# Newton's steps on VectorE for the inverse roots of a kernel's norms, and the last tile's squares summed on TensorE

## The chip, the cores and the metric

One core of a Trainium2 chip runs the whole kernel in one launch. The metric is device time in microseconds (us), the median over several executions. The core's engines are TensorE (PE in the profile; PEld is its weight load), VectorE (DVE), ScalarE (ACT), GpSimd (POOL) and SyncE (SP, which here only starts transfers). Each runs its instructions in order, and they wait for one another through semaphores.

## The reference

Two transformer blocks stand one behind the other, on 512 tokens of width 1024, all in fp32. The first has a chunked attention beside a short convolution, a mixture of 32 experts (two per token), and a gated projection of a side input. The second puts 16 meta tokens in front (528 tokens), and has a pooling mixer, a feed-forward layer, keys and values, a sliding-window attention and another feed-forward layer. What the change touches is the norm, which stands before and behind nearly each of these parts:

```python
def rms_norm(x, g):
    xf = x.astype(jnp.float32)
    y = xf * lax.rsqrt(jnp.mean(xf * xf, axis=-1, keepdims=True) + EPS)
    return (y * g.astype(jnp.float32)).astype(x.dtype)
```

For every token the squares of 1024 numbers are averaged, and the token is multiplied by the inverse root of that mean. The kernel does the matmuls of the large weights in three parts each (high and low halves of weights and data).

## The kernel before

**Layout.** Activations lie transposed: 8 tiles of 128 features, each with the tokens as columns (`hT`, `yT`: 128 x 8 x 528). Tokens are worked on in two halves, r = 0 and 1, of 272 and 256 columns (of 256 and 256 behind the meta tokens' last use). Weights stream through `raw` (SyncE's transfers), are cast to `whi` by ScalarE (L1675) and split to `wlo` by VectorE (L971); `tile` (L377) makes three matmuls for each piece (L388).

**A norm over features.** The features of a token are spread over partitions and tiles, so a norm (name `nm`, half `r`) takes a chain over all four engines:

1. ScalarE squares tile k as it comes (`square`, L1917), the first tile into the accumulator `zacc`, the others into one of three buffers `zsq`.
2. GpSimd adds each buffer to `zacc` (`accumulate`, L2199; L2204); for the second half of the pooling output VectorE does it (L1381).
3. TensorE sums `zacc` over partitions: for each 128 tokens one matmul against a column of ones (`columns`, L690, L697). The trace shows it as two instructions per column. The first half has three columns where the meta tokens are in it, else two.
4. VectorE makes the mean (L1395). ScalarE takes the square root (`root_act`, L355). VectorE takes the reciprocal (L345) and corrects it by one of Newton's steps, four small instructions (L347 to L353; `root`, L342). All of these work on 128 x 2 to 128 x 5 numbers.
5. VectorE writes the roots on a diagonal (L1401, L1402), TensorE spreads them over all partitions (`spread`, L700; L707 for the 16 meta tokens, L709 for the rest), ScalarE copies them to `rb` (L1972).
6. VectorE scales `yT` by `rb` (L1420), GpSimd (r = 0, L2262) or VectorE (r = 1, L1425) adds it to `hT`, ScalarE and VectorE make the high and low halves of the next matmul's input (L1964, L1430).

The fourteen norms of this kind are, by name, `mp0` (pooling output), `fp0` (before the first feed-forward), `fo0` (its output), `kv` (before the keys), `mp1` (attention output), `fp1` and `fo1`, with two halves each. Beside them there are the first norm of the input, by token, with four roots (`x`, L990), the router's (`n2`), the gate's (`ple`, its spread is L653) and the one before the pooling (`pre0`, whose roots scale a matrix, L1336, that TensorE uses at L683). That makes 21 roots. The attention's head norms take a square root of their own on ScalarE (L1714), which stays.

**Order.** Each engine's program is written out by hand. The main stream is the tiles of matmuls; the norms' steps are generators in a list (`Side`) that are advanced once per piece of a tile, so that a few matmuls stand between a column sum and its spread. Since each engine is in order, a step that waits stops all that stands behind it. On ScalarE, each change between a square root, an exponential, a sigmoid and Silu (L1990) puts a table load in front of the instruction.

Of the kernel before, what the change touches and what calls it, by code (L numbers as in the profile page):

```python
# [140 lines left out]
def _program(nc, ctx, T, out, marks):  # L141
# [119 lines left out]
    zsq = [pl(f"zsq{i}", [128, 272]) for i in range(3)]  # L261
    tmp = [pl(f"ztmp{i}", [128, 272]) for i in range(3)]
# [79 lines left out]
    def root(e, w, y, xm, u, name, *event):  # L342

        w.wait_ge(*at("sqrt", *event))
        e.reciprocal(y, y).then_inc(*hit(name))  # L345
        w.wait_ge(*last(name))
        e.tensor_tensor(u, y, y, ALU.mult).then_inc(*hit(name))  # L347
        w.wait_ge(*last(name))
        e.tensor_tensor(u, u, xm, ALU.mult).then_inc(*hit(name))
        w.wait_ge(*last(name))  # L350
        e.tensor_scalar(u, u, -0.5, 1.5, ALU.mult, ALU.add).then_inc(*hit(name))
        w.wait_ge(*last(name))
        e.tensor_tensor(y, y, u, ALU.mult).then_inc(*hit(name, ("root", *event)))  # L353

    def root_act(e, w, y, xm, *event):  # L355
        w.wait_ge(*at("mean", *event))
        e.activation(y, xm, ACT.Sqrt).then_inc(*hit("act_root", ("sqrt", *event)))
# [3 lines left out]
    def tensor(e):  # L361
# [328 lines left out]
        def columns(nm, r):  # L690

            c0 = RNG[nm][r][0]
            b = take(("col", nm, r), SIDE)
            w.wait_ge(*at("acc", nm, r, 7))
            for x, c in CH[r].items():
                if c >= c0:
                    p = e.matmul(b[:, x:x + 1], zacc[:, c:c + 128], ones[:, 0:1], start=True, stop=True)  # L697
            p.then_inc(*hit("pe_norm", ("col", nm, r)))
# [263 lines left out]
    def vector(e):  # L962
# [399 lines left out]
        def dve_pool():  # L1362
# [16 lines left out]
            accumulate("mp0", 1, 7)  # L1379
# [283 lines left out]
    def scalar(e):  # L1663
        w, side = per_engine(e)
        fed, nsq = [0], [0]
        sq_user = {}
# [17 lines left out]
        def act_load():  # L1684
# [4 lines left out]
            for i in range(4):  # L1689
                w.wait_ge(*at("x", i))  # L1690
                e.activation(xr[:, i, :], xt[:, i, :], ACT.Square, accum_out=xs[:, 1, i:i + 1]).then_inc(
                    *hit("act_sq", ("x sq", i)))
                root_act(e, w, xs[:, 0, i:i + 1], xs[:, 1, i:i + 1], "x", i)
# [120 lines left out]
        def act_route():  # L1814
# [8 lines left out]
            root_act(e, w, ns[:, 3, 0:4], ns[:, 2, 0:4], "n2")  # L1823
# [47 lines left out]
        def act_ple():  # L1871
# [18 lines left out]
            for m in range(8):  # L1890
                tile(J["pg"], m)
                if m == 0:
                    root_act(e, w, rcol[:, 0, 1:5], rcol[:, 1, 1:5], "ple")
                    w.wait_ge(*at("prb"))
                    e.copy(rb[:, MT:L], bk("prb")).then_inc(*hit("act_out", ("free", "prb"), ("ple rb",)))
# [9 lines left out]
            root_act(e, w, rcol[:, 0, 0:5], rcol[:, 1, 0:5], "pre0")  # L1905
# [11 lines left out]
        def square(nm, r, k, src, acc, sq):  # L1917

            c0, c1 = RNG[nm][r]
            if k == 0:  # L1920
                e.activation(acc[:, c0:c1], src[:, k, c0:c1], ACT.Square).then_inc(*hit("act_sq", ("acc", nm, r, 0)))
                return
# [27 lines left out]
        def act_post(nm, r, nev, g, off):  # L1950
# [3 lines left out]
            n0, n1 = cols(nm, r)  # L1954
            root_act(e, w, rcol[:, 0, n0:n1], rcol[:, 1, n0:n1], nm, r)
# [18 lines left out]
        def act_rooted(nm, r, wait):  # L1974
            for _ in range(wait):
                yield
            n0, n1 = cols(nm, r)
            root_act(e, w, rcol[:, 0, n0:n1], rcol[:, 1, n0:n1], nm, r)
            yield
            yield  # L1980
            rb_copy(nm, r)
# [214 lines left out]
    def gpsimd(e):  # L2196
# [56 lines left out]
        def pool_post(nm, r, nev):  # L2253
# [4 lines left out]
            for s in range(11):  # L2258
# [5 lines left out]
                if nev and 3 <= s < 10:  # L2264
                    accumulate(nev, r, s - 2, zacc, zsq)
                yield

        def pool_ffn(l, after):
# [7 lines left out]
            for r in range(2):  # L2276
                for m in range(8):
                    tile(J["fd", l, 1, r], m)
                    if m:
                        accumulate(f"fo{l}", r, m, zacc, zsq)  # L2280
# [66 lines left out]
        for k in range(1, 8):  # L2347
# [9 lines left out]
        for r in range(2):  # L2357
            for m in range(8):
                tile(J["wo2b", r], m)
                if m:  # L2360
# [190 lines left out]
```

## Time and profile before

| | |
|---|---|
| Time, median of 3 runs | 2228.89 us (2228.74 to 2229.91) |
| The profiled execution's own time | 2229.37 us |
| Its span, first to last instruction | 2227.6 us |
| Mean granted TensorE clock | 0.931 of full speed |
| TensorE busy | 1905.9 us, 86% of the span |
| VectorE busy | 849.0 us, 38% |
| ScalarE busy | 654.2 us, 29% |
| GpSimd busy | 240.2 us, 11% |

The profile is one execution. A share of busy time is an average over stages: from about 500 to 1000 us the experts' weights are transferred at some 400 GB/s and TensorE waits for them; in the rest it is TensorE's matmuls, stopped at times by a norm. In a list of waits the numbers are the total, how often, and the longest. In a timeline a row gives start and duration in us, engine, line, operation, output<-input, and in brackets how long the engine had been idle before it and what ended that.

### The profile page before, as it was taken

Reading aid. Unit: us, or ns where it says so; the run is one execution under the profiler, and the core shown is the slowest. Engines: PE = TensorE matmul, PEld = TensorE weight load, DVE = VectorE, ACT = ScalarE, POOL = GpSimd, SP = SyncE. Lnnn points to the kernel's source line nnn. Section 1 sums busy time; section 2 is a strip of 40 time slices with the busy share of each in tenths; the row PEclk is TensorE's granted clock in tenths of the full one; section 3 lists DMA queues with packets and bytes.
Section 4 is the critical chain, followed back from the end, with each engine's and each line's share of the span. In section 5 each row is a group of like instructions: output and inputs, shape, how many; then the busy total and the mean of one; then the engine's idle time right before and its main releaser. Section 6 shows DMA issues by size and latency. Waiting matters only on the chain.

```text
span 2227.6 us, 30483 instructions
## 1 busy us (share of the span) xinstructions
PE 1905.9 (86%) x13042; PEld 1563.1 (70%) x13042; DVE 849.0 (38%) x1433; ACT 654.2 (29%) x1195; POOL 240.2 (11%) x235
## 2 busy tenths in 40 slices
PE   6977999959877788767859999998978869999997
PEld 4754888635434334335759999997956759999997
DVE  4644325330000000006583332346655473432455
ACT  5333323301000000014453222234445543222233
POOL 0022000000000000002240000004212240000013
PEclk9998999969999989997979999998999979999998
DMA  6211342649999999984112332233311212232342
GB/s 217 85 48 48 97 170 85 272 145 401 398 395 394 394 405 407 402 335 147 57 38 67 93 98 85 91 97 120 111 39 57 68 56 81 93 104 84 95 141 87
DMA packets 64428, 368.09 MB, mean 165 GB/s; under 512 B 7665, under 2 KB 10353, under 8 KB 52001
## 3 DMA queue, kind: packets, MB, share of 16 engines
q1 hardware_dynamic: 52672, 335.57, 41.4%
q0 software_dynamic: 6032, 21.32, 2.9%
q10 hardware_dynamic: 5584, 9.21, 1.1%
q8 instruction: 105, 1.72, 0.3%
q14 instruction: 35, 0.28, 0.0%
HBM read 349.55 MB, written 16.52 MB: 164 GB/s over the span
## 4 chain that ended last, share of the span: by engine, by line
PE 62%; DMA 19%; DVE 10%; ACT 5%; POOL 2%; issue 2%; SPq 0%; POOLq 0%; ACTq 0%; DVEq 0%
PE bank L388 49%; DMA e<-in_we 17%; PE bank L563 3%; PE bank L581 2%; POOL zacc L2204 1%; ACT SS L2098 1%; PE bank L434 1%; DVE scr L1135 1%; DMA yg<-y_scratch,dst 1%; PE bank L709 1%; DVE SS L1563 1%; DVE sm L1570 1%; DVE ztmp L1420 1%; PE bank L774 1%; PE bank L816 1%
## 5 line engine op out<-in xcount | busy, mean ns | idle before, releaser
L388 PE MATMUL bank<-nhi,whi 128*128 128x256 f32 (+2 forms) x1568 | 457.4, 292 | 14.4 <-DVE nlo L1430 6.6
L388 PE MATMUL bank<-nlo,whi 128*128 128x256 f32 (+2 forms) x1568 | 452.0, 288 | 0.0
L388 PE MATMUL bank<-nhi,wlo 128*128 128x256 f32 (+2 forms) x1568 | 451.9, 288 | 0.0
L971 DVE TENSOR_TENSOR wlo<-raw,whi 128x1024 fp32r<-128x1024 f32 x243 | 304.3, 1259 | 143.8 <-ACT whi L1675 140.0
L388 PEld LDWEIGHTS bank<-nhi,whi 128*128 128x128 f32 x1568 | 303.3, 193 | 19.9 <-DVE yT L1615 7.0
L388 PEld LDWEIGHTS bank<-nlo,whi 128*128 128x128 f32 x1568 | 302.9, 193 | 0.9
L388 PEld LDWEIGHTS bank<-nhi,wlo 128*128 128x128 f32 x1568 | 302.1, 193 | 1.5
L1675 ACT CAST whi<-raw 128x1024 fp32r<-128x1024 f32 x243 | 252.9, 1042 | 143.0 <-PE bank L388 118.5
L563 PE MATMUL bank<-e,xT 128*64 128x256 f32 x2048 | 245.1, 394 | 48.0 <-DMA e<-in_we 38.3
L563 PEld LDWEIGHTS bank<-e,xT 128*64 128x64 f32 x2048 | 151.9, 142 | 146.9 <-DMA e<-in_we 53.9
L388 PE MATMUL bank<-ghi,whi 128*128 128x256 f32 (+1 forms) x704 | 202.5, 288 | 0.0
L388 PE MATMUL bank<-ghi,wlo 128*128 128x256 f32 (+1 forms) x704 | 200.9, 285 | 0.0
L388 PE MATMUL bank<-glo,whi 128*128 128x256 f32 (+1 forms) x704 | 200.7, 285 | 0.0
L1266 DVE TENSOR_TENSOR hb<-hb,bank 128x256 f32<-128x256 f32 x32 | 13.5, 421 | 465.2 <-PE bank L563 465.2
L581 PE MATMUL bank<-e,h 128*64 128x512 f32 x512 | 136.3, 682 | 50.0 <-DMA e<-in_we 49.4
L2204 POOL TENSOR_TENSOR zacc<-zacc,zsq 128x256 f32<-128x256 f32 (+1 forms) x91 | 90.3, 993 | 818.1 <-ACT zsq L1929 816.9
L388 PEld LDWEIGHTS bank<-ghi,whi 128*128 128x128 f32 x704 | 135.6, 193 | 0.0
L388 PEld LDWEIGHTS bank<-glo,whi 128*128 128x128 f32 x704 | 135.4, 192 | 0.0
L388 PEld LDWEIGHTS bank<-ghi,wlo 128*128 128x128 f32 x704 | 135.1, 192 | 0.0
L581 PEld LDWEIGHTS bank<-e,h 128*64 128x64 f32 x512 | 39.4, 154 | 131.1 <-issue 69.0
L388 PE MATMUL bank<-xhi,whi 128*128 128x512 f32 x288 | 122.2, 424 | 3.2 <-DVE wlo L971 3.2
L388 PE MATMUL bank<-xhi,wlo 128*128 128x512 f32 x288 | 114.4, 397 | 0.0
(305 smaller groups left out, 2530.7 us busy)
## 6 DMA issues: line engine op xcount, KB each, us to landing
e<-in_we SPq DMA_DIRECT2D x96, 2048.0 KB, 46.4
raw<-in_w_down SPq DMA_DIRECT2D x64, 512.0 KB, 3.6
raw<-in_w_gate SPq DMA_DIRECT2D x44, 512.0 KB, 3.5
raw<-in_w_up SPq DMA_DIRECT2D x44, 512.0 KB, 3.5
y_scratch<-ys ACTq DMA_DIRECT2D x64, 128.0 KB, 8.4
raw<-in_w_q SPq DMA_DIRECT2D x12, 512.0 KB, 4.0
B<-in_rel POOLq DMA_DIRECT2D x8, 512.0 KB, 4.4
raw<-in_w_gc SPq DMA_DIRECT2D x8, 512.0 KB, 4.1
```

The source lines that it names most:

```text
L388: i = e.matmul(o, a, x[:, k0 + k, c0:c1], start=(k == 0 and n == 0), stop=(k == j.K - 1 and n == 2))
L434: p = e.matmul(bs[i][:, 0:256], x[:, k, t], a, start=(k == 0 and n == 0), stop=(k == 7 and n == 2))
L563: p = e.matmul(b[64 * hf:64 * hf + 64, 0:256], xT[n % 2][:, k, :], W[:, k, 256 * hf:256 * hf + 256], start=(k == 0), stop=(k == 7))
L581: p = e.matmul(b[64 * nh:64 * nh + 64, :], h2[n % 2][:, 2 * (kc % 2) + kc // 2, :], W[:, kc, 512 * nh:512 * nh + 512], start=(kc == 0), st ...
L709: p = e.matmul(b[:, o + (i - m0) * 128:o + (i - m0 + 1) * 128], ones, dg[:, i - 1, :], start=True, stop=True)
L774: p = e.matmul(b[:, 0:128], x[:, k, c:c + 128], a, start=(k == 0 and n == 0), stop=(k == 7 and n == 2))
L816: p = e.matmul(bb[par][:, x * 256 + c0:(x + 1) * 256], qT[64 * par:64 * par + 64, h // 2, t * 128:(t + 1) * 128], kT[64 * par:64 * par + 6 ...
L971: e.tensor_tensor(wlo[u % NSP][:], raw[u % NRAW][:], whi[u % NSP][:].bitcast(F32), ALU.subtract).then_inc(*hit("dve_low", ("lo", u)))
L1135: op(*a, **kw).then_inc(*hit("dve_route", *ev))
L1420: e.scalar_tensor_tensor(x[:, 0:c1 - c0], yT[:, s, c0:c1], v1(name, 8 * l + s), rb[:, c0:c1], ALU.mult, ALU.mult).then_inc(*hit("dve_post" ...
L1675: e.copy(whi[u % NSP][:], raw[u % NRAW][:]).then_inc(*hit("act_high", ("hi", u)))
L2204: e.tensor_tensor(a, a, sq[marks.noted("sq", nm, r, k)][:, 0:c1 - c0], ALU.add).then_inc(*hit("pool_acc", ("acc", nm, r, k)))
```

## The change

Two things. The square root on ScalarE and the reciprocal go; `root` now starts from an integer estimate of the inverse root (the bits of the mean, halved and taken from a constant) and makes three of Newton's steps, of three instructions each, all on VectorE, at all 21 roots. And in the fourteen norms over features, ScalarE writes the squares of the eighth tile to one of two new buffers `zlast`, nobody adds them to `zacc`, and TensorE takes them in with a second matmul per column. `pre0`, which has its own accumulator, keeps its additions.

```diff
+    zlast = [pl(f"zlast{i}", [128, 272]) for i in range(2)]
...
     def root(e, w, y, xm, u, name, *event):
-        w.wait_ge(*at("sqrt", *event))
-        e.reciprocal(y, y).then_inc(*hit(name))
-        w.wait_ge(*last(name))
-        e.tensor_tensor(u, y, y, ALU.mult).then_inc(*hit(name))
-        w.wait_ge(*last(name))
-        e.tensor_tensor(u, u, xm, ALU.mult).then_inc(*hit(name))
-        w.wait_ge(*last(name))
-        e.tensor_scalar(u, u, -0.5, 1.5, ALU.mult, ALU.add).then_inc(*hit(name))
-        w.wait_ge(*last(name))
-        e.tensor_tensor(y, y, u, ALU.mult).then_inc(*hit(name, ("root", *event)))
-
-    def root_act(e, w, y, xm, *event):
         w.wait_ge(*at("mean", *event))
-        e.activation(y, xm, ACT.Sqrt).then_inc(*hit("act_root", ("sqrt", *event)))
+        e.tensor_scalar(y.bitcast(I32), xm.bitcast(I32), -0.5, 1597463007.0, ALU.mult, ALU.add).then_inc(*hit(name))
+        for n in range(3):
+            w.wait_ge(*last(name))
+            e.tensor_tensor(u, y, y, ALU.mult).then_inc(*hit(name))
+            w.wait_ge(*last(name))
+            e.scalar_tensor_tensor(u, u, -0.5, xm, ALU.mult, ALU.mult).then_inc(*hit(name))
+            w.wait_ge(*last(name))
+            e.scalar_tensor_tensor(y, u, 1.5, y, ALU.add, ALU.mult).then_inc(
+                *hit(name, *([("root", *event)] if n == 2 else [])))
...
         def columns(nm, r):
             c0 = RNG[nm][r][0]
             b = take(("col", nm, r), SIDE)
-            w.wait_ge(*at("acc", nm, r, 7))
+            w.wait_ge(*at("acc", nm, r, 6))
+            w.wait_ge(*at("sq", nm, r, 7))
+            sq = zlast[marks.noted("last", nm, r)]
             for x, c in CH[r].items():
                 if c >= c0:
-                    p = e.matmul(b[:, x:x + 1], zacc[:, c:c + 128], ones[:, 0:1], start=True, stop=True)
+                    e.matmul(b[:, x:x + 1], zacc[:, c:c + 128], ones[:, 0:1], start=True, stop=False)
+                    p = e.matmul(b[:, x:x + 1], sq[:, c - c0:c - c0 + 128], ones[:, 0:1], start=False, stop=True)
...
         def square(nm, r, k, src, acc, sq):
+            if k == 7 and nm != "pre0":
+                i = len(lasts) % 2
+                if len(lasts) >= 2:
+                    w.wait_ge(*at("col", *lasts[-2]))
+                lasts.append((nm, r))
+                marks.note(i, "last", nm, r)
+                e.activation(zlast[i][:, 0:c1 - c0], src[:, k, c0:c1], ACT.Square).then_inc(
+                    *hit("act_sq", ("sq", nm, r, k)))
+                return
...
-            root_act(e, w, rcol[:, 0, n0:n1], rcol[:, 1, n0:n1], nm, r)
...
-                if nev and 3 <= s < 10:
+                if nev and 3 <= s < 9:
                     accumulate(nev, r, s - 2, zacc, zsq)
...
-                    if m:
+                    if 1 <= m < 7:
                         accumulate(f"fo{l}", r, m, zacc, zsq)
```

`root_act` goes at all its six call sites. The additions of tile 7 go in the same way at the other three places (VectorE's for `mp0`, GpSimd's for `mp0` and `mp1`). The steps in the `Side` lists stay where they were.

## Rows read from the trace of the kernel before

**Rows 1.** List of waits, whole span: who waited for whom: total, times, longest.
```profile
PE bank L709 <- DVE dg L1402: 25.2, 10, 9.4
PE bank L697 <- POOL zacc L2204: 22.8, 8, 7.5
PE bank L404 <- DVE xr L990: 17.0, 1, 17.0
...
PE bank L707 <- DVE dg L1402: 11.1, 3, 7.8
...
PE bank L683 <- DVE Wr L1336: 3.6, 1, 3.6
...
PE bank L653 <- DVE dg L1346: 2.2, 1, 2.2
...
PE bank L388 <- DVE sl L1458: 1.2, 2, 0.6
```

**Rows 2.** Timeline of the last norm (fo1, second half), near the end of the kernel.
```profile
2211.57 0.72 POOL L2204 TENSOR_TENSOR zacc<-zacc,zsq 128x256 f32<-128x256 f32 x1 [2.80 <-ACT zsq L1929]
...
2212.43 0.58 PE L697 MATMUL bank<-cst,zacc 128*128 128x1 f32 x4 [2.31 <-POOL zacc L2204]
2213.05 0.16 DVE L1395 TENSOR_SCALAR rcol<-bank 128x2 f32<-128x2 f32 x1 [2.01 <-PE bank L697]
2213.24 0.20 ACT L357 ACTIVATE rcol<-rcol 128x2 f32<-128x2 f32 x1 [1.75 <-DVE rcol L1395]
2213.48 0.17 DVE L345 RECIPROCAL rcol<-rcol 128x2 f32<-128x2 f32 x1 [0.27 <-ACT rcol L357]
...
2214.47 0.42 DVE L1402 TENSOR_TENSOR dg<-cst,rcol 128x256 f32<-128x256 f32 x1
...
2215.04 1.19 PE L709 MATMUL bank<-dg,cst 128*128 128x128 f32 x4 [2.03 <-DVE dg L1402]
```

**Rows 3.** Groups by line and form, VectorE: busy us, mean ns, idle before.
```profile
L1135 DVE SCALAR_TENSOR_TENSOR scr<-scr 128x4 f32<-128x4 f32 x2 | 0.3, 164 | 0.1
```

**Rows 4.** Groups by line, ScalarE: its table loads for root and Silu.
```profile
L357 ACT ACT_TABLE_LOAD x9 | 11.5, 1283 | 0.2
...
L1990 ACT ACT_TABLE_LOAD x4 | 5.1, 1283 | 0.1
```

**Rows 5.** Timeline of fo0's first half: the last addition and the column sums.
```profile
1527.80 1.21 POOL L2204 TENSOR_TENSOR zacc<-zacc,zsq 128x272 f32<-128x272 f32 x1 [2.55 <-ACT zsq L1929]
...
1529.15 0.80 PE L697 MATMUL bank<-cst,zacc 128*128 128x1 f32 x6 [1.78 <-POOL zacc L2204]
```

**Rows 6.** Timelines of kv's first half and mp1's second half, GpSimd and TensorE.
```profile
1549.14 2.65 POOL L2204 TENSOR_TENSOR zacc<-zacc,zsq 128x272 f32<-128x272 f32 x2
...
1551.94 1.41 PE L697 MATMUL bank<-cst,zacc 128*128 128x1 f32 x6 [7.49 <-POOL zacc L2204]
...
1803.91 5.93 POOL L2204 TENSOR_TENSOR zacc<-zacc,zsq 128x256 f32<-128x256 f32 x5 [0.24 <-ACT zsq L1929]
...
1809.90 1.01 PE L697 MATMUL bank<-cst,zacc 128*128 128x1 f32 x4 [4.82 <-POOL zacc L2204]
```

**Rows 7.** Timeline of fp0's second half, with a table load before the root.
```profile
1180.22 1.28 ACT L357 ACT_TABLE_LOAD   x1
1180.23 0.16 DVE L1395 TENSOR_SCALAR rcol<-bank 128x2 f32<-128x2 f32 x1 [3.71 <-PE bank L697]
...
1182.75 0.42 DVE L1402 TENSOR_TENSOR dg<-cst,rcol 128x256 f32<-128x256 f32 x1
```

**Rows 8.** Timeline of fp0's first half: VectorE beside GpSimd, before the mean.
```profile
1162.21 0.47 DVE L1430 SCALAR_TENSOR_TENSOR nlo<-hT,vec,nhi 128x256 fp32r<-128x256 f32 x1
...
1164.54 2.20 DVE L1430 SCALAR_TENSOR_TENSOR nlo<-hT,vec,nhi 128x256 fp32r<-128x256 f32 x3
...
1165.54 0.91 POOL L2204 TENSOR_TENSOR zacc<-zacc,zsq 128x256 f32<-128x256 f32 x1 [0.35 <-ACT zsq L1929]
```

**Rows 9.** Busy time by stretch; the last three columns: PEclk, DMA share, GB/s.
```profile
1138.00:1151.00 13.00, 5.75 (x19) 4.38 (x19) 12.27 (x19) 5.67 (x14) 10.34 (x12) 0.50 0.03 5
```

More of the change, by code:

```diff
@@ L1378, in dve_pool @@
                     accumulate("mp0", 1, m - 1)
-            accumulate("mp0", 1, 7)
         def accumulate(nm, r, k):
@@ L1665, in scalar @@
         fed, nsq = [0], [0]
-        sq_user = {}
+        sq_user, lasts = {}, []
         def feed(top):
@@ L1692, in act_load @@
                     *hit("act_sq", ("x sq", i)))
-                root_act(e, w, xs[:, 0, i:i + 1], xs[:, 1, i:i + 1], "x", i)
             w.wait_ge(*at("vec"))
@@ L1822, in act_route @@
                                      *hit("act_sq", *([("n2 sq",)] if i == 3 and hf else [])))
-            root_act(e, w, ns[:, 3, 0:4], ns[:, 2, 0:4], "n2")
             w.wait_ge(*at("root", "n2"))
@@ L1892, in act_ple @@
                 if m == 0:
-                    root_act(e, w, rcol[:, 0, 1:5], rcol[:, 1, 1:5], "ple")
                     w.wait_ge(*at("prb"))
@@ L1904, in act_ple @@
             side.drain()
-            root_act(e, w, rcol[:, 0, 0:5], rcol[:, 1, 0:5], "pre0")
         def act_by_token(g):
@@ L1953, in act_post @@
             yield
-            n0, n1 = cols(nm, r)
-            root_act(e, w, rcol[:, 0, n0:n1], rcol[:, 1, n0:n1], nm, r)
             yield
@@ L1976, in act_rooted @@
                 yield
-            n0, n1 = cols(nm, r)
-            root_act(e, w, rcol[:, 0, n0:n1], rcol[:, 1, n0:n1], nm, r)
             yield
@@ L2346, in gpsimd @@
                 accumulate("pre0", r, k, qacc, qsq)
-        for k in range(1, 8):
+        for k in range(1, 7):
             accumulate("mp0", 0, k, zacc, zsq)
@@ L2359, in gpsimd @@
                 tile(J["wo2b", r], m)
-                if m:
+                if 1 <= m < 7:
                     accumulate("mp1", r, m, zacc, zsq)
```

## The prediction

> **What bounds the kernel now.** I read the list of waits first, since the change touches only short steps. In it TensorE sits idle in front of the spread of a norm's roots (L709, and L707 where the 16 extra columns come first) for 25.2 and 11.1 us, thirteen of the fourteen times that a norm is taken column by column, and in front of the column sums (L697) for 22.8 us, eight times, waiting for GpSimd's last addition [rows 1]. Its instructions run in order, so whatever makes the chain from the last square to the spread longer stops all matmuls behind it. Next the timeline of the last norm, to see that chain link by link [rows 2]: GpSimd adds the eighth tile's squares, TensorE sums the columns 0.86 us after that addition began, VectorE makes the mean at 2213.05, ScalarE takes a square root of two columns in 0.20 us, five VectorE instructions from L345 on take 0.99 us together, the diagonal (L1402) starts at 2214.47 and TensorE's spread follows it. From mean to diagonal: 1.42 us. Outside the mixture of experts, where weights' transfers are the limit, this pattern of chain and stop returns at every norm.
>
> **The change, part by part.**
>
> *The root.* It loses ScalarE's step and its five VectorE instructions and gets ten. Five cost 0.99 us, 0.20 each with the hand-over [rows 2]; the new kind, two tensors and a scalar, takes 164 ns on four columns [rows 3], as the old ones do. So from the mean to the diagonal 0.20 + 10 x 0.20 = 2.20 us, against 1.42: **+0.78 us** wherever no table load lay between. For the integer form of the first instruction the trace has no row on a few columns; between the 0.16 us of the rows beside it and twice that, I take 0.2.
>
> *The column sums.* Each column gets a second matmul pair. Six instructions take 0.80 us [rows 5], four 0.58 [rows 2]: 0.11 each by the difference, 0.145 by the quotient; I take 0.13. So +0.8 us for the norms with three columns, +0.5 for two, and where the clock stands at its lower level, as in rows 6, +1.3 and +1.0.
>
> *The last addition.* TensorE can begin when GpSimd now begins: −0.86 us at the end of the kernel [rows 2], −1.35 where VectorE splits weights beside it [rows 5]. ScalarE's eighth square has the same size and goes to another buffer; the wait it gains is for a column sum two norms back, long done. Behind it on ScalarE would stand casts of weights, if it weren't.
>
> *Norm by norm* (the last addition, the extra sums, the root):
> - First half of both feed-forward outputs, second half of the first, first half of the attention output, TensorE waiting for an addition of 1.2 us as in rows 5: −1.3 + 0.5 (once 0.8) + 0.78, about zero each, together +0.3.
> - The last norm −0.86 + 0.5 + 0.78 = +0.4, and the pooling output's first half, with 0.8 for the sums, +0.8: together +1.2.
> - Two where GpSimd has a queue [rows 6]. At 1551.94 two additions take 2.65 us; one goes: −1.0 + 1.3 + 0.8 = +1.1. At 1809.90 five take 5.93 us, 1.19 each; the first and the last of them go. That gives back between one and two, 1.2 to 2.4 us; I take 2.05, since only the last square's lateness can eat into it: −2.05 + 1.0 + 0.8 = −0.25. Together +0.9.
> - Three where TensorE doesn't wait for the sum. In rows 7 a table load lay between mean and diagonal, 2.52 us; it becomes 2.20: −0.3 + 0.5 = +0.2. Its like in the second layer had only part of the load there: +0.45. The keys' second half has none: +0.5 + 0.8 = +1.3. Together +2.0.
> - Three where VectorE itself is late and reaches the mean without waiting [rows 8]: root +0.78, sums hidden. But there the last addition ran beside VectorE's work: one such instruction takes 0.47 us alone, and three take 2.20 beside GpSimd. Without it I take 0.45 back: +0.33 each, +1.0.
>
> Fourteen norms: 0.3 + 1.2 + 0.9 + 2.0 + 1.0 = **+5.4 us**.
>
> *Roots outside these.* The gate's, the pooling's and the first norm of the input have TensorE waiting behind them (2.2, 3.6 and, at the start, 17.0 us [rows 1]): +0.78 each, +2.3. The first norm's four roots no longer stop ScalarE, but only the last tile's counts. The router's root loses an exposed load and gains as much: nothing.
>
> *Table loads.* Nine loads of 1.28 us for the square root go, and two of the four for Silu, which followed them [rows 4]; one comes back for the attention's head norms, which still take a square root. Those for the root are in the sums above, or fell in ScalarE's idle time. The two Silu loads stand ahead of a 0.59 us stop of TensorE each, 1.2 us together [rows 1]; that is what they return: **−1.2 us**. If part of the load stays hidden, less; with a full 1.28 each, −2.6.
>
> The sum: 5.4 + 2.3 − 1.2 = **+6.5 us** on the profiled execution's 2229.37, so 2235.9; the median of the runs shown is 0.48 below that execution, so I say **2235.4 us**, 0.3% slower.
>
> The trace shows what a load costs by itself: at 1180.22 it takes 1.28 us, and the root that follows it comes to its diagonal 1.10 us later than without one [rows 2, 7]. The Trainium skill (ScalarE: Activation LUTs, What ACT_TABLE_LOAD costs) has it dearer, 1.28 us plus 1.38 of draining, 2.66 for every switch. Ten fewer switches would be an estimated 26.6 us by that page, and the change would win.
>
> **The rivals.**
> 1. *Sharing between VectorE and GpSimd is worth more* (the other side). Place: every last addition, beside which VectorE's instructions take about twice as long [rows 8]. Fourteen additions each slow two instructions by 0.48 us: 13.4 us, of which 1.35 is counted; 12 more give 2223. It decides from thirteen such instructions on (6.5/0.48). Against it: in eight of the norms VectorE only waits for TensorE's sum at that time, and has nothing to speed up.
> 2. *Loads cost more than their row.* If each of the ten held the path for its whole 1.28 us, 12.8 us would return, of which some 4 are counted: 2227; with as long again behind each, 2214. Against it: most loads fell in ScalarE's waits, and in rows 7 the 2.52 us are the load's 1.28 and a root's 1.24, with no room for more. The page named above has the dearer form.
> 3. *TensorE's clock.* While it worked in short bursts with stops between, the granted clock was 0.50, its 1.2 GHz level, from 1138 to 1151 [rows 9]. Longer stops at each norm could start one or two such stretches more; a stretch of 10 us of matmuls at that level costs 5 us: 2240. For it: stops grow in about ten places. Against: by under 1.3 us each, and others shrink.
> 4. *The change does less than it says.* The filler matmuls between sum and spread cover the longer root. They did not cover even the shorter one in thirteen of fourteen cases [rows 1], so a cover can be hoped for in four places at most, 3.1 us less: 2232, no measurable change.
>
> **How the numbers follow.** My case 0.74, rival 1 0.08, rival 2 0.02, rival 3 0.12, rival 4 0.04. In my case the least is +3 us (sums at 0.11 an instruction, Silu loads in full, more relief in the queue at 1551.94), the most +10 (a first instruction twice as long, sums at 0.145, no relief from sharing, nothing for Silu): 2232 to 2239. A measurement of this kernel can tell about 0.2%, 4.5 us, from no change, so the border is at 2233.4; about 0.18 of my case lies below it and 0.56 above. Slower: 0.56 + 0.12 = 0.68; the same: 0.18 + 0.04 = 0.22; faster: 0.10. The range reaches down over part of rival 4 and up to rival 3: 2229.5 to 2240.
>
> **What would show it.** In the profile after: 2.2 us from each mean to its diagonal, with ten VectorE instructions at 0.20; twelve and eight matmuls in the column sums; TensorE's 22.8 us before them down to about 11 to 13; its waits for L709 and L707 up by some 8 to 10; ten table loads fewer, one before the first head norm; no Silu load behind the second half's roots, and there no stop of 0.59 us. I am wrong if the waits before the spread don't grow, if the ten instructions take other than 2 us, or if stages with no norm in them change.

## The result and the profile after

The changed kernel takes **2233.22 us** in the median (2230.45 to 2240.67) where the kernel before takes 2228.89: a ratio of 1.0021, 95% interval 1.0012 to 1.0030, so 4.7 us slower, clear of no change by its interval and just at the 4.5 us that the prediction took as the least that can be told. The forecast was 2235.4 us, +6.5 on the profiled execution. The profiled executions differ by exactly that, 2235.87 against 2229.37, which is partly luck: a second set of runs of the same kernel gave 2233.28 and a ratio of 1.0022.

From the page of the kernel after, the busy time of each engine and the slices of the granted clock:

```profile
PE 1919.8 (86%) x13106; PEld 1572.3 (70%) x13106; DVE 863.3 (39%) x1537; ACT 636.8 (29%) x1164; POOL 227.6 (10%) x222
...
PEclk9998999969999889997879999998999969999998
```

Its list of waits, the lines that answer to [rows 1]:

```profile
PE bank L709 <- DVE dg L1401: 27.9, 10, 8.1
PE bank L401 <- DVE xr L990: 17.7, 1, 17.7
PE bank L707 <- DVE dg L1401: 13.0, 4, 7.5
PE bank L696 <- POOL zacc L2204: 11.3, 2, 7.9
...
PE bank L696 <- ACT zlast L1924: 4.0, 5, 1.5
```

TensorE's idle time ahead of the spreads grew from 36.3 to 40.9 us; ahead of the column sums it fell from 22.8 to 15.3, of which GpSimd still ends 11.3 in two cases, the two with a queue [rows 6]. So 7.5 us of one wait went and 4.6 of another came, and the kernel is slower all the same: doubled sums count as busy, and so does work at the lower clock.

The last norm, the chain of [rows 2] in its new form (timeline):

```profile
2217.16 0.42 ACT L1924 ACTIVATE zlast<-yT 128x256 f32<-128x256 f32 x1 [3.11 <-DVE yT L1504]
...
2217.72 0.35 PE L696 MATMUL bank<-cst,zacc 128*128 128x1 f32 x2 [1.51 <-ACT zlast L1924]
...
2217.94 0.36 PE L697 MATMUL bank<-cst,zlast 128*128 128x1 f32 x2
...
2218.78 0.16 DVE L1394 TENSOR_SCALAR rcol<-bank 128x2 f32<-128x2 f32 x1 [1.65 <-PE bank L697]
2218.98 0.17 DVE L346 TENSOR_SCALAR rcol<-rcol 128x2 int32<-128x2 int32 x1
2219.18 0.16 DVE L349 TENSOR_TENSOR rcol<-rcol 128x2 f32<-128x2 f32 x1
2219.38 0.16 DVE L351 SCALAR_TENSOR_TENSOR rcol<-rcol 128x2 f32<-128x2 f32 x1
...
2220.75 0.16 DVE L353 SCALAR_TENSOR_TENSOR rcol<-rcol 128x2 f32<-128x2 f32 x1
2220.95 0.43 DVE L1401 TENSOR_TENSOR dg<-cst,rcol 128x256 f32<-128x256 f32 x1
...
2221.52 1.19 PE L709 MATMUL bank<-dg,cst 128*128 128x128 f32 x4 [2.78 <-DVE dg L1401]
```

GpSimd is gone from the chain: the sums start 0.14 us after ScalarE's square ends. From the first sum to the mean is 1.06 us (0.62 before), from the mean to the diagonal 2.17 (1.42 before): ten instructions 0.195 apart, ScalarE not among them.

ScalarE's table loads, groups by line, against [rows 4]: the nine of the root are gone, two of the four for Silu, and one came, ahead of the first head norm.

```profile
L1990 ACT ACT_TABLE_LOAD x2 | 2.6, 1283 | 0.0
...
L1712 ACT ACT_TABLE_LOAD x1 | 1.3, 1283 | 0.0
```

### The profile page after: what moved, and what is told of

Its sections match the earlier page's. It is cut to its first block, busy times and chain, and to the rows that moved or that the text cites. A ratio compares the mean times of both kernels' runs of the same rounds, so it can differ in the third digit from the quotient of the medians.

```text
span 2234.1 us, 30652 instructions
## 1 busy us (share of the span) xinstructions
PE 1919.8 (86%) x13106; PEld 1572.3 (70%) x13106; DVE 863.3 (39%) x1537; ACT 636.8 (29%) x1164; POOL 227.6 (10%) x222
## 4 chain that ended last, share of the span: by engine, by line
PE 61%; DMA 18%; DVE 11%; ACT 4%; issue 3%; POOL 2%; another core or an unknown queue 0%; ACTq 0%; DVEq 0%; POOLq 0%; SPq 0%
PE bank L385 48%; DMA e<-in_we 16%; PE bank L560 4%; PE bank L578 2%; ACT SS L2098 1%; PE bank L431 1%; DVE scr L1135 1%; POOL zacc L2204 1%; DVE SS L1562 1%; DVE sm L1569 1%; PE bank L709 1%; DVE wlo L971 1%; PE bank L816 1%; DVE ztmp L1419 1%; PE bank L774 1%
## 5 line engine op out<-in xcount | busy, mean ns | idle before, releaser
L560 PE MATMUL bank<-e,xT 128*64 128x256 f32 x2048 | 257.4, 409 | 60.1 <-DMA e<-in_we 47.7
L2204 POOL TENSOR_TENSOR zacc<-zacc,zsq 128x256 f32<-128x256 f32 (+1 forms) x78 | 78.0, 1000 | 818.8 <-ACT zsq L1933 818.1
L385 PE MATMUL bank<-xlo,whi 128*128 128x512 f32 x288 | 114.4, 397 | 0.0
```

Of the source, the lines that this page charges most:

```text
L385: i = e.matmul(o, a, x[:, k0 + k, c0:c1], start=(k == 0 and n == 0), stop=(k == j.K - 1 and n == 2))
L560: p = e.matmul(b[64 * hf:64 * hf + 64, 0:256], xT[n % 2][:, k, :], W[:, k, 256 * hf:256 * hf + 256], start=(k == 0), stop=(k == 7))
L2204: e.tensor_tensor(a, a, sq[marks.noted("sq", nm, r, k)][:, 0:c1 - c0], ALU.add).then_inc(*hit("pool_acc", ("acc", nm, r, k)))
```

## The experiments

Ratios are against the kernel before, run on the same chip beside each group of experiments (medians 2228.53, 2229.34 and 2228.25 us); 0.1% is 2.2 us. Twelve kernels in three groups.

### Group 1: the two halves, and the table loads alone

**after_again** is the changed kernel unaltered.

> The changed kernel once more, to part what belongs to it from what belongs to one execution. Theory A (the chains of the norms alone): 3 to 6 us over the kernel before; in the profile the stages without a norm (the experts, the gathering of their rows, the sliding-window attention) lie within 1.5 us of before, either way, and differ from the first profile of this kernel, where the experts and the gather took 3.3 us more. Theory B (the change slowed the experts' stage too, by the shifted start of its transfers): those 3.3 us are there again, with the same sign.

Measured: 2233.28 us, ratio 1.0022 (1.0010 to 1.0033). It is the yardstick for what follows. The time is what theory A says; its 1.5 us for stages without a norm are not. The experts' stage, from its first matmul to its last, took 509.1 us before, 510.6 after and 511.4 here, and sliding-window attention is 3.9 us shorter here than before. Over all fourteen profiles the experts' stage takes 506.4 to 511.7 us, and the longest is that of no_switch, whose roots are no longer than before's. So theory B isn't borne out either: a difference of 2 us in that stage tells nothing of an edit.

**root_only** is the kernel before with the new root alone: `root` as in the diff, all `root_act` removed, the last square still added by GpSimd.

> The new root alone; the last addition stays with GpSimd and VectorE. Theory A: 0.74 us from mean to diagonal more at twelve norms, the gate's and the pooling's root, 0.63 at the input's, less 0.35 and 0.08 at the two norms that had a table load before the root, less 1.2 for the two Silu loads: 10 us slower than before, between 8 and 12. Theory B: the root costs 5 to 6 us, and the rest of the change's loss stands in the experts' stage, whichever half is taken.

Measured: 2238.82 us, ratio 1.0042 (1.0028 to 1.0056): +9.4 us.

**last_only** is the other half: the last square summed on TensorE, the old root kept.

```diff
-            w.wait_ge(*at("acc", nm, r, 7))
+            w.wait_ge(*at("acc", nm, r, 6))
+            w.wait_ge(*at("sq", nm, r, 7))
+            sq = zlast[marks.noted("last", nm, r)]
```

> The eighth tile's squares on TensorE alone, with the square root on ScalarE as before. Theory A: four norms gain 0.7 to 0.9 us each, the last one 0.4, the one with five additions in the queue 1.2, the three where VectorE is late 0.45 each; the keys' norms lose 0.3 and 0.4: 5 to 6 us faster than before. Rival: the longer column sums and the shorter addition cancel, as 0.44 to 1.3 us against 0.8 to 1.3: within 2 us of before.

Measured: 2222.90 us, ratio 0.9979 (0.9968 to 0.9990): −4.7 us. **The halves add**: +0.42 − 0.21 = +0.21%, which is the whole. The change joins something that helps to something that costs twice as much. Theory A holds for root_only (8 to 12 us); last_only lies just under its 5 to 6 us and further from its rival's 2, with an interval from −7.1 to −2.2.

**no_switch** is the kernel before, with the loads taken away and the time of the root kept. ScalarE copies instead of taking the root, and VectorE's reciprocal becomes an integer estimate of the inverse root, so there is the same number of instructions on both engines and nine loads fewer (the roots of x and n2 keep theirs). What it leaves out is accuracy: one Newton step on an estimate, about 0.2% off.

```diff
-        e.reciprocal(y, y).then_inc(*hit(name))
+        if event[0] in ("x", "n2"):
+            e.reciprocal(y, y).then_inc(*hit(name))
+        else:
+            e.tensor_scalar(y.bitcast(I32), y.bitcast(I32), -0.5, 1597463007.0, ALU.mult, ALU.add).then_inc(*hit(name))
...
-        e.activation(y, xm, ACT.Sqrt).then_inc(*hit("act_root", ("sqrt", *event)))
+        e.activation(y, xm, ACT.Sqrt if event[0] in ("x", "n2") else ACT.Copy).then_inc(*hit("act_root", ("sqrt", *event)))
```

> The kernel before with nine table loads less and every instruction else of the same kind and length: for 16 of the 21 roots ScalarE copies the mean instead of taking its root, and VectorE's reciprocal becomes the integer estimate (with the one step of Newton's that follows, the roots are then good to some 0.2%). What loads cost the path: Theory A, only what was seen exposed (1.1 and 0.8 us ahead of two roots, 0.6 behind each of two more): 3 us faster. Rival, each load held the path for its 1.28 us: 11.5 faster. Rival of the page that has 2.66 us a switch: 24 faster.

Measured: 2222.10 us, ratio 0.9972 (0.9961 to 0.9983): −6.2 us. Twice what theory A said, half of the 11.5 us that the first rival said and a quarter of the dearest price. The surplus can be seen at the second half of the first feed-forward input's norm (fp0). Timeline of the kernel before, the continuation of [rows 7]:

```profile
1181.51 0.21 ACT L357 ACTIVATE rcol<-rcol 128x2 f32<-128x2 f32 x1
...
1183.32 0.96 PE L709 MATMUL bank<-dg,cst 128*128 128x128 f32 x4 [2.31 <-DVE dg L1402]
...
1184.29 0.41 PE L388 MATMUL bank<-nlo,whi 128*128 128x256 f32 x1
```

and of no_switch, the same instructions:

```profile
1184.27 0.68 PE L712 MATMUL bank<-dg,cst 128*128 128x128 f32 x4 [1.21 <-DVE dg L1405]
...
1184.91 0.28 PE L391 MATMUL bank<-nlo,whi 128*128 128x256 f32 x1
```

The load itself costs what its row says: the root begins at 1181.51, 10 ns after a load that started at 1180.22 and took 1.28, with nothing drained between. But TensorE stopped for 2.31 us with the load and 1.21 without, and behind the longer stop each matmul of 256 columns takes 0.41 us instead of 0.28. The four microseconds behind the spread, busy time by stretch (the last three columns: granted clock, DMA share, GB/s), first before, then no_switch:

```profile
1183.30:1187.30 4.00, 3.98 (x21) 4.00 (x22) 1.01 (x1) 1.39 (x2) 0.00 (x0) 0.57 0.39 131
```

```profile
1184.30:1188.30 4.00, 4.00 (x34) 4.00 (x35) 2.07 (x2) 1.42 (x2) 0.00 (x0) 1.00 0.45 127
```

21 matmuls against 34 in the same time. The clock stood near 0.5, the 1.2 GHz level, in the one and at 2.4 GHz in the other. The changed kernel has no load there, but its ten instructions make the stop 1.96 us, and it too goes on at the lower level:

```profile
1189.87 1.19 PE L709 MATMUL bank<-dg,cst 128*128 128x128 f32 x4 [1.96 <-DVE dg L1401]
...
1191.08 0.41 PE L385 MATMUL bank<-nlo,whi 128*128 128x256 f32 x1
```

The traces of before and no_switch can be laid over each other: for the same matmul, how much later does it start in the one than in the other? From the pooling output's norm to the end no_switch gains on before in two places alone, 3.5 us around the second half of fp0's norm and 3.2 around that of fp1, its like in the second feed-forward layer; at the other twelve norms the two traces move against each other by less than 0.3 us. The two gains fall into three parts each: the stop is shorter by 1.1 and 0.8 us, the matmuls behind it win 1.5 each by the clock, and the two missing Silu loads give back 0.8 each. Together that is 1.9 + 3.1 + 1.7 = 6.7 us, against 6.2 by the medians.

So a **theory C** came up that the prediction had as rival 3, with a chance of 0.12: the stop's length is paid once as a stop, and sometimes again as a stretch at 1.2 GHz behind it. The next group tests the slope and the clock separately.

### Group 2: the root longer and shorter, the sums reordered, the stop filled

**five_steps** and **one_step** change the number of Newton's steps in the changed kernel.

```diff
-        for n in range(3):
+        for n in range(5):
```

> The changed kernel with five of Newton's steps instead of three in every root: six more instructions on VectorE, 1.17 us by the spacing of 0.195 us in the changed kernel's trace, at about 18 roots (14 of the output norms, four of the others). Theory A (a longer root comes out whole, at nearly every norm): 1.17 x 14 to 18 = 16 to 21 us slower than the changed kernel, 2249 to 2255. Rival (waits and filler work take up about half of it, as rival 4 of the prediction had it): 8 to 10 us slower, 2242. Theory C (a longer stop of TensorE also costs clock, beyond its own length): more than 22 us.

Measured: 2262.67 us, ratio 1.0149 (1.0132 to 1.0167), 1.27% or 28.3 us above the changed kernel.

```diff
+        steps = 3 if event[0] in ("x", "n2") else 1
-        for n in range(3):
+        for n in range(steps):
```

> The changed kernel with one step in place of three in all roots except the two ahead of the experts (x and n2 keep three): the root's relative error grows to about 0.2% there. Six instructions less, 1.17 us, at 16 roots. Theory A (the roots lie on the path, no other work is hidden behind them): 14 to 19 us faster than the changed kernel, 2214 to 2219. Rival (the spare time is taken by the next latest, the second-half preparation on ScalarE or the weights' low parts on VectorE): 7 to 10 us faster, 2224 to 2226. It stands against five_steps: with a straight line between them the two differ by the same amount from the changed kernel.

Measured: 2209.24 us, ratio 0.9909 (0.9892 to 0.9926), 25.2 us below the changed kernel. Both rivals with hidden roots are out: nothing covers a root here. The lists of waits of five_steps and one_step, the spreads with no extra columns:

```profile
PE bank L709 <- DVE dg L1401: 40.3, 10, 9.9
```

```profile
PE bank L710 <- DVE dg L1402: 16.0, 8, 7.0
```

In the traces each place where a root stands moves the rest of the kernel by about the full 1.18 us of its six instructions. At the start of the kernel five_steps is late by 4.5, for the roots of the four input tiles lie in a row; n2, ple, pre0 and each of the 14 norms add theirs. Own length: 21 places, 24.6 us for five_steps; 16 places, 18.9 for one_step. Measured are 28.3 and 25.2, that is 1.15 and 1.33 times the instructions' own time. Theory A had at most 21 and 19. For five_steps part of the difference is my own miscount of the places (18 for 21), so that the bound of 22 for theory C was set too low; what is left in both is a surplus of 4 to 6 us over the instructions' own time, hardly more than these intervals, but of the same sign twice. The table of places at the end of this section shows where it sits.

**sums_first** issues the sums over the running sum ahead of the wait for the last square.

```diff
-            w.wait_ge(*at("sq", nm, r, 7))
-            for x, c in CH[r].items():
-                if c >= c0:
-                    e.matmul(b[:, x:x + 1], zacc[:, c:c + 128], ones[:, 0:1], start=True, stop=False)
-                    p = e.matmul(b[:, x:x + 1], sq[:, c - c0:c - c0 + 128], ones[:, 0:1], start=False, stop=True)
+            todo = [(x, c) for x, c in CH[r].items() if c >= c0]
+            for x, c in todo:
+                e.matmul(b[:, x:x + 1], zacc[:, c:c + 128], ones[:, 0:1], start=(x == todo[0][0]), stop=False)
+            w.wait_ge(*at("sq", nm, r, 7))
+            for x, c in todo:
+                p = e.matmul(b[:, x:x + 1], sq[:, c - c0:c - c0 + 128], ones[:, 0:1], start=False,
+                             stop=(x == todo[-1][0]))
```

> The changed kernel with the order of the column sums changed: the two or three matmuls over the running sum stand ahead of the wait for the eighth square, the two or three over the square behind it. By the rows of the column sums (0.67 us more with three columns, 0.44 with two) up to half of the sums is taken ahead of the square: if the doubled sums are what is on the path, 0.3 to 0.6 us at each of the 12 norms whose square comes last, 3.5 to 7 us faster (2226 to 2230). Rival: the running sum itself (GpSimd's sixth addition, to which 11.3 us of the wait ahead of the sums is put down in 2 of the cases) is as late as the square, and the order gives under 1.5 us.

Measured: 2229.27 us, ratio 0.9999 (0.9989 to 1.0009): 5.1 us below the changed kernel, give or take 3.4, inside the first theory's range, and level with the kernel before. Its last norm, timeline:

```profile
2212.98 0.50 PE L695 MATMUL bank<-cst,zacc 128*128 128x1 f32 x4
...
2214.10 0.42 ACT L1926 ACTIVATE zlast<-yT 128x256 f32<-128x256 f32 x1 [3.11 <-DVE yT L1506]
2214.56 0.61 PE L698 MATMUL bank<-cst,zlast 128*128 128x1 f32 x4 [1.08 <-ACT zlast L1926]
2215.21 0.16 DVE L1396 TENSOR_SCALAR rcol<-bank 128x2 f32<-128x2 f32 x1 [1.15 <-PE bank L698]
```

From the end of the eighth square to the mean it takes 0.69 us where the changed kernel takes 1.20. That is won at six norms, not at the twelve that were expected: 0.2 to 0.7 us each, 3.2 together. At the others nothing is won: at two GpSimd's running sum comes last, as the rival said of them, and at six TensorE comes to the sums late or VectorE to the mean. The other 2 us of the 5.1 lie within the interval.

**keep_busy** fills TensorE's stop.

```diff
             o = MT if n0 == 0 else 0
+            if nm != "kv" and nm != "fo0":
+                for _ in range(7):
+                    e.matmul(b[:, 0:128], ones, ident, start=True, stop=True)
             w.wait_ge(*at("diag", nm, r))
```

> The changed kernel with seven more 128-column matmuls (constants by constants, into the bank that the spread takes, overwritten by it) issued just ahead of the wait for the root, in all norms except kv and fo0, so that TensorE works through most of its stop of about 2 us. The results are the same. Theory C (the stops during the roots bring the granted clock down for a stretch behind them, and that is part of the price): less time at the lower clock around 1140 to 1200, 1810 to 1850 and at the end, 3 to 6 us faster. Rival (the clock falls for other stops, or not for these): 0 to 2 us slower, since at the lower clock seven matmuls outlast the root.

Measured: 2227.82 us, ratio 0.9996 (0.9985 to 1.0006): **5.8 us faster than the changed kernel, give or take 3.5, with 70 useless matmuls more**. Timeline and stretch of the same place in keep_busy:

```profile
1185.45 1.72 PE L707 MATMUL bank<-cst 128*128 128x128 f32 x14
1187.47 0.71 PE L712 MATMUL bank<-dg,cst 128*128 128x128 f32 x4 [0.29 <-DVE dg L1404]
...
1188.14 0.28 PE L385 MATMUL bank<-nlo,whi 128*128 128x256 f32 x1
```

```profile
1187.40:1191.40 4.00, 3.93 (x33) 3.93 (x34) 2.13 (x3) 1.42 (x2) 0.00 (x0) 1.00 0.43 119
```

The seven matmuls (x14, since each is recorded in two parts) are done 0.29 us before the spread starts, the spread starts when it would have anyway, and the clock stays at 2.4 GHz: 33 matmuls in the four microseconds, against 22 at a granted clock of 0.60 behind the spread of the changed kernel. From the window mixing to the first full pass of the feed-forward, 100 us that hold the first layer's four output and input norms, the granted clock is 0.78 in the changed kernel and 0.87 here:

```profile
1111.00:1211.00 100.00, 75.19 (x524) 72.94 (x523) 63.28 (x142) 43.65 (x92) 23.17 (x26) 0.78 0.13 43
```

```profile
1110.00:1210.00 100.00, 83.16 (x608) 80.93 (x607) 65.25 (x144) 45.29 (x94) 23.19 (x26) 0.87 0.13 43
```

### Group 3: is the surplus the clock, does the kernel before pay it too, and what comes of it all

**five_busy** is five_steps with twelve such matmuls a norm in place of keep_busy's seven.

> five_steps with twelve more 128-column matmuls ahead of the wait for each root (kv and fo0 excepted), as keep_busy has seven. five_steps stood 27 to 29 us above the changed kernel, where six instructions of 0.195 us at 21 places in a row (four of the input's roots, n2, ple, pre0 and 14 norms) are 24.6. Theory C (the 3 to 4 us over this, and the 5 to 6 us that keep_busy won, are time of TensorE at the lower clock behind its stops): 24 to 25 us above keep_busy, about 2252, and 9 to 11 below five_steps. Rival (the surplus is other work that the longer root pushes, not the clock): 27 to 29 us above keep_busy, 2256, 6 below five_steps.

Measured: 2255.49 us, ratio 1.0120 (1.0103 to 1.0138). That is 6.5 us below five_steps and 27.6 above keep_busy, on the rival's side; the profiled spans are 24.0 apart (2248.8 and 2224.8), on theory C's. The intervals are 4 us wide each way, and the profile is of the fastest of its four runs, so the totals don't decide it. Filling the stops wins about the same, 6 us, with a root of 2.2 us and of 3.3. The places one by one, below, do decide it where stops were filled.

**before_busy** is the kernel before with four such matmuls a norm.

> The kernel before with four more 128-column matmuls ahead of the wait for each root (kv and fo0 excepted); its root takes 1.42 us. Theory C (every stop during a root costs clock, the shorter one too): 3 to 4 us faster than before, 2225 to 2226, so of the changed kernel's root only the surplus of 0.74 us a norm is new and most of the clock was lost before too. Rival (only the longer stop brings the clock down): within 1 us of before.

Measured: 2226.82 us, ratio 0.9989 (0.9976 to 1.0002): −2.5 us, between the two, with an interval from −5.4 to +0.4 us. Of the total no more can be said. In its trace the second halves of fp0 and fp1 each pass 1.7 and 1.6 us faster than before: the kernel before pays for the clock there too.

**two_first_busy** and **one_first_busy** put the parts together: fewer steps, sums_first's order, and the filled stop.

```diff
-        for n in range(3):
+        for n in range(2):
...
+                for _ in range(5):
+                    e.matmul(b[:, 0:128], ones, ident, start=True, stop=True)
```

> The changed kernel with two steps in every root (seven instructions, relative error about 0.0005%), the sums over the running sum ahead of the wait for the square, and five more 128-column matmuls ahead of the wait for the root. If the parts add: the changed kernel 2234, less 13 (one step, half of the 25 that one_step won with two), less 4.5 (sums_first), less 4 to 5 (a shorter stop has less clock to win back than keep_busy's 6) = 2211 to 2213. If they take from each other (the shorter root already wins most of the clock back): 2216 to 2218.

Measured: 2211.52 us, ratio 0.9920 (0.9906 to 0.9933).

> one_step (one step in all roots but x and n2, relative error about 0.2%) with the sums over the running sum ahead of the wait for the square and three more 128-column matmuls ahead of the wait for the root. If the parts add: 2209 less 4.5 less 2 to 3 = 2202. If a stop of 1 us costs no clock any more, the matmuls are worth nothing or push the spread back: 2205.

Measured: 2202.34 us, ratio 0.9878 (0.9861 to 0.9895). Both land where the parts add. two_first_busy is the version to keep: 0.8% faster than the kernel before and 1.0% faster than the changed one, with roots still good to about 0.0005%. one_first_busy has 0.4% more, for roots that are 0.2% off.

### The places, one by one

Four spreads have TensorE at 2.4 GHz for the 5 us ahead of the stop in all these profiles but one (before_busy at the last place), so what the stop does can be read behind them. Each cell has the stop ahead of the spread in us, and the granted clock of the 5 us from the spread's start (1.00 is 2.4 GHz throughout, 0.50 is 1.2 GHz throughout; "none" is a spread that follows the matmul before it at once).

| run | fp0, second half | fp1, second half | mp1, first half | fo1, first half |
|---|---|---|---|---|
| before | 2.31, 0.66 | 2.04, 0.66 | 0.87, 0.66 | 1.16, 0.66 |
| no_switch | 1.21, 1.00 | 1.21, 1.00 | 0.77, 0.66 | 1.14, 0.66 |
| before_busy | 1.32, 1.00 | 1.05, 1.00 | none, 1.00 | none, 0.73 |
| after | 1.96, 0.68 | 1.96, 0.66 | 1.52, 0.69 | 1.86, 0.66 |
| root_only | 1.95, 0.66 | 1.95, 1.00 | 1.51, 0.50 | 1.87, 0.72 |
| sums_first | 1.95, 0.66 | 1.95, 0.68 | 1.50, 1.00 | 1.87, 0.66 |
| keep_busy | 0.29, 1.00 | 0.29, 1.00 | none, 1.00 | 0.30, 1.00 |
| one_step | 0.77, 1.00 | 0.78, 1.00 | 0.34, 1.00 | 0.69, 1.00 |
| five_steps | 3.12, 0.50 | 3.13, 0.68 | 2.70, 0.50 | 3.04, 0.50 |
| five_busy | 0.37, 1.00 | 0.37, 1.00 | none, 1.00 | 0.37, 1.00 |

In the changed kernel the clock falls at all four, in keep_busy and one_step at none. But the length of this one stop doesn't decide it. 1.95 us brought the clock down five times in six, and left it up behind fp1 in root_only; 0.77 and 0.87 us brought it down at mp1, where TensorE had stopped another time just before, ahead of the column sums. The kernel before there:

```profile
1781.54 0.61 PE L697 MATMUL bank<-cst,zacc 128*128 128x1 f32 x4 [1.17 <-POOL zacc L2204]
...
1784.17 1.11 PE L709 MATMUL bank<-dg,cst 128*128 128x128 f32 x4 [0.87 <-DVE dg L1402]
```

And what each place cost, in us, by the start of the last matmul ahead of the next norm's sums:

| pair | fp0, second half | fp1, second half | fo1, first half |
|---|---|---|---|
| keep_busy against after | −1.6 | −1.6 | −1.3 |
| one_step against after | −2.7 | −2.7 | −2.5 |
| five_steps against after | +2.1 | +1.1 | +2.2 |
| five_busy against keep_busy | +1.2 | +1.2 | +1.2 |

The six instructions are 1.2 us. With the clock up in both (the last row) they cost just that. The kernel one_step wins 1.3 to 1.5 us more, for it also keeps the clock up; and five_steps loses 0.9 to 1.0 more at the two places where its granted clock is lower than the changed kernel's, and nothing more where it is the same. So at these places the surplus over a root's own length is the clock. Over the whole kernel it is shown in sign alone.

## Why the prediction was right

**The total** was +6.5 us against +4.3 to +4.7, inside the range, on the right side, by terms that were not all right. By halves, as the prediction's own terms split: the last addition with its sums −3.9 forecast, −4.7 measured (last_only); root and loads +10.2 forecast (the prediction's sums are rounded up by 0.2), +9.4 measured (root_only). Both held.

**The root.** 2.20 us from mean to diagonal forecast, 2.16 measured in the norms with two or three columns; +0.78 a place forecast, +0.74 measured. The integer first instruction takes 0.17 us, at the cheap end of its bounds. That nothing hides it (against rival 4) is shown by five_steps and one_step.

**The column sums.** Forecast +0.8 for three columns, +0.5 for two, +1.3 and +1.0 at the lower clock; measured +0.67, +0.44, +1.3 and +0.86. An added instruction (a matmul is two in the trace) costs 0.11 us, the difference of the two rows and not their quotient.

**Where the profiled 6.5 us stand** is in part luck. In the profile of the changed kernel 5.3 us of them are there before the first of the fourteen norms, in after_again's 4.4, where the prediction has 2.3 for the roots of the input, the gate and the pooling; 1.5 and 2.3 us of this came in the experts' stage, which wanders by more than that between profiles. From there to the end, sliding-window attention left out, both profiles lose 3.6 us on before, where the prediction has 5.4 − 1.2 = 4.2.

**The price of a stop was put at the stop's own length**, and that step failed, though it didn't show in the total. Of the loads the prediction counted 3.1 us in the places that no_switch changes: 1.1 and 0.8 ahead of the two exposed roots, and 1.2 ahead of Silu. The trace has the first two as forecast, 1.7 for the Silu loads, and 3.1 more for which the prediction had nothing: TensorE at 1.2 GHz behind the two stops. The longer root was charged at its length in 17 places, 13.3 us, where the difference of root_only and no_switch is 15.6; the interval is 4 us wide each way, so this size isn't shown to be wrong, and the two errors can't be said to cancel to the last. The prediction saw the clock at 0.50 in [rows 9], called it rival 3, and set against it that the stops grow "by under 1.3 us each". It did not see that the kernel before already had such a stretch behind other stops: at the second halves of fp0 and fp1 the kernel before pays for a stop with the load and the changed kernel for one with ten instructions, and both go on at the lower clock, so little of it shows in their difference. That the total held in spite of this is luck too.

**The waits.** The forecast for L709 and L707 was 8 to 10 us more; it was 4.6. In root_only they grew by 8.0, as forecast, from 36.3 to 44.3:

```profile
PE bank L705 <- DVE dg L1398: 29.9, 10, 9.5
...
PE bank L703 <- DVE dg L1398: 14.4, 4, 9.0
```

and last_only took 2.2 away (24.0 and 10.1): I had not thought that the other half would touch this wait. The wait ahead of the sums fell to 15.3, not to 11 to 13.

**Norm by norm**, where both profiles agree, the forecast was good: the pooling output's first half +0.9 us for +0.8, the keys' second half +1.2 at its spread for +1.3, the last norm +0.4 for +0.4. Around the first feed-forward output's first half, the keys' first half and the output's second half, which follow each other, the changed kernel stands at −1.3, +3.6 and −1.2 us against before and after_again at −0.7, +2.0 and −1.4: the stretches at 1.2 GHz lie differently there in each profile, and what one of these norms costs can't be read from a pair.

**Rivals.** Rival 1, more relief from VectorE and GpSimd apart, falls: last_only returned 4.7, not 12 more. Its price was too high from the start: in [rows 8] three instructions take 2.20 us beside GpSimd and would take 1.4 alone, so 0.8 us for an addition and not 2 x 0.48. Rival 2 falls in both forms. With nine loads gone for 1.28 us each it would be 11.5 us, and no_switch measured 6.2 (3.8 to 8.7), of which loads by themselves are 3.6. The load that [rows 7] show starts 20 ns behind a cast on ScalarE, and the root starts 10 ns behind the load: no draining shows on either side. The prediction's sentence on the Trainium skill (ScalarE: Activation LUTs, What ACT_TABLE_LOAD costs) meets the trace here: by the Trainium skill's 2.66 us a switch, nine would be an estimated 24 us, and the trace doesn't agree. Rival 3 was right as a mechanism and wrong in where it stands: the clock is lost before the change too. Rival 4 falls by five_steps and one_step.

**Stages with no norm in them** did change, which the prediction had named as a sign against itself. Sliding-window attention, from the spread of the keys' second half to the column sums behind it, took 170.7 us before, 168.3 after and 166.8 in after_again, the same kernel. Stretches of root_only and keep_busy:

```profile
1616.40:1790.10 173.70, 146.70 (x897) 109.88 (x898) 85.97 (x180) 85.59 (x244) 35.73 (x25) 0.90 0.17 52
```

```profile
1614.10:1780.90 166.80, 141.64 (x897) 106.23 (x898) 85.86 (x180) 84.70 (x244) 34.58 (x24) 0.94 0.17 53
```

The work is the same, 897 matmuls. The granted clock differs, 0.90 at 173.7 us, 0.91 in last_only at 173.1, 0.94 in before, after and keep_busy, and with it TensorE's busy time; between before (170.7) and after_again (166.8) it is TensorE's idle time, 29.1 and 23.6 us. Nothing of the change is in this stretch. The same kernel's two profiles are 1.5 us apart and different kernels' up to 7, so it is either scatter of single executions or a matter of where in time an edit makes the stretch begin; what tips it was not tried. Either way a difference of a few microseconds in one profile's stage is no measure of an edit, and medians of several runs are.

## What to carry to other kernels

In a kernel that TensorE bounds, a chain of tiny instructions between two of its matmuls costs its whole length and, where it tips the clock, 1.3 to 1.5 us more; count its instructions at 0.2 us each, and ask first how many steps the accuracy needs. Look for work that can go ahead of the wait (half of the column sums here: 3 us in the trace, 5 in the medians) and, if a stop of about 2 us stays, try filling it with matmuls into a bank about to be overwritten. When a change has two halves, time each alone: here one was worth keeping by itself.

## What the runs showed of the hardware

- At the second half of fp0's norm the granted clock stayed at 2.4 GHz after a stop of 1.21 us (no_switch) or 1.32 us (before_busy); after 1.96 us (the changed kernel) and 2.31 us (before) it stood at 1.2 GHz for some 3 us from about the spread's start, and matmuls of 256 columns took 0.41 us instead of 0.28. In root_only, after 1.95 us, it fell just over 1.5 us later. The length of one stop doesn't settle it: elsewhere it fell after 0.77 us and stayed up after 1.95 (the table above).
- A table load took 1.283 us; the one in [rows 7] began 20 ns behind the cast ahead of it, and the activation behind it 10 ns later.
- VectorE's instructions on 128 x 2 values take 0.16 to 0.17 us whatever they do (tensor by tensor, two tensors and a scalar, integers), and follow each other in 0.195 when each waits for the one before.
- Matmuls with one column of output cost 0.11 us for each of their two recorded instructions at the upper clock (+0.44 us for four, +0.67 for six) and about 0.21 at the lower (+0.86 for four).
